# Three input projections as products of 512 columns, and two side jobs moved in the first experts of a mixture-of-experts layer

## The reference

```
h    = layer_norm(concat(meta, x))
proj = h @ w_in                          # q, k, v, og, a1, z, xbc, dt
gla  = rms_norm(gla_chunk_causal(q, k, v, log_a)) * silu(og)
ssd  = rms_norm((ssd_chunk_causal(...) + xs * d) * silu(z))
h    = layer_norm(alpha * h + concat(gla, ssd) @ w_out)
# top 4 of 32 experts per token; per expert e, for its tokens:
hid  = clamped_swiglu(x @ w_gate[e] + b_gate[e], x @ w_up[e] + b_up[e])
y   += gate * (hid @ w_down[e] + b_down[e])
out  = layer_norm(alpha * h + y)[:, 16:]
```

## Time and profile before

| | us |
|---|---|
| median of 3 runs | 1059.09 |
| the three runs | 1060.35, 1058.22, 1059.09 |
| the profiled execution | 1058.86 |
| its span in the profile | 1057.0 |
| TensorE busy | 1021.6 |
| VectorE busy | 228.6 |
| ScalarE busy | 143.9 |
| mean granted clock of TensorE | 0.991 |
| moved from HBM | 424.59 MB, 403 GB/s over the span |

### The profile page before, as it was taken

The page is one execution under the profiler, slowest core; times in us unless marked ns, Lnnn a source line. Parts: engine busy times, 40 slices in busy tenths (PEclk is TensorE's granted clock), DMA queues, the critical chain, the costliest instruction groups (busy, mean ns, idle before and its releaser), DMA issues.

```text
span 1057.0 us, 12137 instructions
## 1 busy us (share of the span) xinstructions
PE 1021.6 (97%) x5116; PEld 449.5 (43%) x5116; DVE 228.6 (22%) x495; ACT 143.9 (14%) x348; POOL 29.7 (3%) x50
## 2 busy tenths in 40 slices
PE   8999999999999999999999999999999999999997
PEld 7888764333333333333333333333333333333332
DVE  5453572111111111111111112211111111111112
ACT  3312331111111111011110111111111110011102
POOL 1230100000000000000000000000000000000000
PEclk9999999999999999999999999999999999999999
DMA  9894689999999999999999999999999999999995
GB/s 314 273 410 192 201 327 410 428 428 435 429 429 435 432 425 433 435 436 424 430 435 436 424 422 436 432 430 426 435 434 428 428 435 435 430 425 427 428 418 236
DMA packets 40011, 426.21 MB, mean 403 GB/s; under 512 B 6922, under 2 KB 19347, under 8 KB 23204
## 3 DMA queue, kind: packets, MB, share of 16 engines
q1 hardware_dynamic: 37940, 424.12, 95.6%
q10 hardware_dynamic: 2032, 1.53, 0.6%
HBM read 424.59 MB, written 1.05 MB: 403 GB/s over the span
## 4 chain that ended last, share of the span: by engine, by line
PE 72%; DMA 26%; ACT 1%; DVE 0%; issue 0%; SPq 0%; POOL 0%; DVEq 0%; POOLq 0%; ACTq 0%
PE bank L1200 30%; DMA ring<-in_moe_w_up 18%; PE bank L1251 15%; DMA ring<-in_moe_w_gate 8%; PE bank L1180 4%; PE bank L1172 4%; PE bank L856 3%; PE bank L871 2%; PE bank L1046 2%; PE bank L1034 1%; PE bank L988 1%; PE bank L1242 1%; PE bank L1120 1%; PE bank L949 1%; PE bank L1054 1%; PE bank L1220 1%
## 5 line engine op out<-in xcount | busy, mean ns | idle before, releaser
L1200 PE MATMUL bank<-ring,arena 128*64 128x512 f32 x1988 | 447.5, 603 | 23.8 <-DMA ring<-in_moe_w_up 20.3
L1200 PEld LDWEIGHTS bank<-ring,arena 128*64 128x64 f32 x1988 | 142.5, 139 | 298.7 <-issue 257.7
L1251 PE MATMUL bank<-ring,arena 128*64 128x512 f32 x1024 | 226.8, 595 | 1.5 <-issue 1.5
L1251 PEld LDWEIGHTS bank<-ring,arena 128*64 128x64 f32 x1024 | 71.5, 137 | 151.7 <-issue 150.2
L1641 DVE COPY arena<-bank 128x512 f32<-128x512 f32 x32 | 22.1, 692 | 326.0 <-PE bank L1251 326.0
L741 ACT ACTIVATE arena<-arena 128x512 f32<-128x512 f32 x32 | 20.1, 629 | 451.1 <-DVE arena L1628 451.1
L1180 PE MATMUL bank<-arena 64*128 64x512 f32 x256 | 72.0, 640 | 0.9 <-DVE arena L1641 0.9
L1172 PEld LDWEIGHTS bank<-arena 128*128 128x128 f32 x480 | 58.8, 196 | 22.8 <-issue 22.8
L1635 DVE TENSOR_SCALAR arena<-bank 128x512 f32<-128x512 f32 x32 | 22.1, 692 | 210.3 <-PE bank L1200 210.3
L752 ACT ACTIVATE arena<-bank 128x512 f32<-128x512 f32 x32 | 19.1, 597 | 337.4 <-PE bank L1242 337.4
L1172 PE MATMUL bank<-arena 128*128 128x128 f32 x480 | 64.5, 288 | 0.0
(11 more groups left out here) (281 smaller groups left out, 511.6 us busy)
## 6 DMA issues: line engine op xcount, KB each, us to landing
ring<-in_moe_w_down SPq DMA_DIRECT2D x25, 4096.0 KB, 29.6
ring<-in_moe_w_gate SPq DMA_DIRECT2D x24, 4096.0 KB, 25.4
ring<-in_moe_w_up SPq DMA_DIRECT2D x24, 4096.0 KB, 28.2
ring<-in_moe_w_gate SPq DMA_DIRECT2D x10, 2048.0 KB, 22.6
ring<-in_moe_w_up SPq DMA_DIRECT2D x10, 2048.0 KB, 15.2
ring<-in_moe_w_down SPq DMA_DIRECT2D x10, 2048.0 KB, 17.4
ring<-in_w_in SPq DMA_DIRECT2D x12, 1024.0 KB, 11.8
ring<-in_moe_w_gate SPq DMA_DIRECT2D x8, 1024.0 KB, 17.2
```

The lines of the kernel that those rows point to most:

```text
L1200: ins = mm(b[h * SL:(h + 1) * SL, :], (xA[pp], xB)[q][:, k, par * SL:(par + 1) * SL], columns(unit_at(m, kt), h), start=False, stop=kt == ...
L1251: ins = mm(bank[6][h * SL:(h + 1) * SL, :], hidT[:, kt % 4, (kt // 4) * SL:(kt // 4 + 1) * SL], unit_at(2, kt)[:, h * 512:(h + 1) * 512], ...
```

## The change

Seven edits in one. (1) `v`, `z` and `og` are loaded as 512 columns: the first transfer of a pair brings row groups 0 to 3 of all 512 columns, the second row groups 4 to 7 (`w_wide`); sizes, count and semaphores stay. (2) Their products are made 512 columns wide, 8 per token tile instead of 16 of 256 (`token_wide`); token tile 0 is now complete before tile 1 begins. (3) `meta_rows` reads the wide unit. (4) `counts()` writes bank 7 instead of bank 5. (5) `hidden_bias(0)` of expert 0 stands behind the first gathers instead of ahead of them. (6) `gate_transposes()`, its copy on ScalarE and the wait for it move from expert 0 to expert 3 (`BIASED`). (7) VectorE makes the list behind expert 0's first activation step, and TensorE waits for it behind `hidden(1)`.

```diff
+BIASED = UNROLL - 1
+WIDE = (U_V, U_Z, U_OG)
+        def w_wide(n):
+            return ring[:, n // 4, (n % 4) * HW:(n % 4 + 2) * HW].rearrange("p (k n) -> p k n", k=KT)
...
             for n, c0 in enumerate(W_ORDER):
-                sp.dma_start(w_unit(n), w_in[0, :, c0:c0 + 256].rearrange("(k p) n -> p k n", p=P)).then_inc(w_landed[n], 16)
+                if n in WIDE or n - 1 in WIDE:
+                    u = n if n in WIDE else n - 1
+                    c0, rows = W_ORDER[u], HALVES[n - u]
+                    sp.dma_start(w_wide(u)[:, rows, :], w_in[0, :, c0:c0 + 512].rearrange("(k p) n -> p k n", p=P)[:, rows, :]).then_inc(
+                        w_landed[n], 16)
+                else:
+                    sp.dma_start(w_unit(n), w_in[0, :, c0:c0 + 256].rearrange("(k p) n -> p k n", p=P)).then_inc(w_landed[n], 16)
...
-                if first:
+                if isinstance(n, int) and n == BIASED:
                     act.wait_ge(GT_ps, 1)
                     nc.scalar.activation(GT, bank[7][96:96 + NE, 0:SEQ], ACT.Copy).then_inc(GT_ok, 1)
...
+            def token_wide(out, n, t, kts):
+
+                for kt in kts:
+                    if kt % 4 == 0:
+                        pe.wait_ge(w_landed[n + kt // 4], 16)
+                    ins = mm(out, hT[:, kt, META + t * P:META + (t + 1) * P], w_wide(n)[:, kt, :], start=kt == 0, stop=kt == KT - 1)
+                return ins
...
-            token_major(bank[5][:, 0:256], U_V, 0)
+            token_wide(bank[5][:, :], U_V, 0, first_half)
...
-            token_major(bank[7][:, 0:256], U_V, 1)
+            token_wide(bank[5][:, :], U_V, 0, second_half).then_inc(v_ps, 1)
...
-            pe.wait_ge(w_landed[U_V + 1], 16)
-            for t, b in enumerate((bank[5], bank[7])):
-                token_major(b[:, 256:512], U_V + 1, t).then_inc(v_ps, 1)
-            meta_rows(bank[3][:, 0:HV], HV, [(U_V + g // 2, (g % 2) * HV) for g in range(4)]).then_inc(v_ps, 1)
+            token_wide(bank[7][:, :], U_V, 1, range(KT)).then_inc(v_ps, 1)
+            meta_rows(bank[3][:, 0:HV], HV, w_wide(U_V)).then_inc(v_ps, 1)
...
-            for hf in range(2):
-                n = U_Z + hf
-                pe.wait_ge(w_landed[n], 16)
-                for t in range(NT):
-                    for kt in range(KT):
-                        ins = mm(bank[(0, 5)[t]][:, hf * 256:(hf + 1) * 256], hT[:, kt, META + t * P:META + (t + 1) * P], wslot(n, kt),
-                                 start=kt == 0, stop=kt == KT - 1)
-                    if hf:
-                        ins.then_inc(z_ps, 1)
+            for t in range(NT):
+                token_wide(bank[(0, 5)[t]][:, :], U_Z, t, range(KT)).then_inc(z_ps, 1)
...
+            token_wide(bank[6][:, :], U_OG, 0, range(KT)).then_inc(og_ps, 1)
+            token_wide(bank[7][:, :], U_OG, 1, first_half)
+            pe.wait_ge(mix_y, 2)
+            mix_transposes(bank[0], z_t, (4, 5))
+            mix_transposes(bank[5], z_t, (6, 7))
+            token_wide(bank[7][:, :], U_OG, 1, second_half).then_inc(og_ps, 1)
...
-            hidden_bias(0, bank[4], 0, True)
...
+            hidden_bias(0, bank[4], 0, True)
...
-                    ins = mm(bank[5][0:1, 0:NE], ones_b[:, 0:1], maskb[:, t, :], start=t == 0, stop=t == 1)
+                    ins = mm(bank[7][0:1, SEQ:SEQ + NE], ones_b[:, 0:1], maskb[:, t, :], start=t == 0, stop=t == 1)
...
                 if first:
                     counts()
+                listing = isinstance(n, int) and n == BIASED
+                if listing:
                     gate_transposes()
-                else:
+                if not first:
                     pe.wait_ge(yd_ok, n)
...
-                if first:
-                    pe.wait_ge(list_ok, 1)
...
                 if first:
+                    pe.wait_ge(list_ok, 1)
+                if listing:
                     pe.wait_ge(GT_ok, 1)
...
                 ts(shuffled(a_c, 2), natural(bank[4][:, :], 2), LIMIT, None, ALU.min).then_inc(a_ok, 1)
+                if first:
+                    list_overflow()
```

More of the change, by code:

```diff
@@ L872, in token_major, with meta_rows @@
                 return ins
[L874 removed]
+            def token_wide(out, n, t, kts):
[4 more added lines that the diff above has]
+                return ins
+            def meta_rows(dst, cols, unit):
                 for kt in range(KT):
[L877 to L878 removed]
+                    for g, m in enumerate(MH):
+                        ins = mm(dst[m, :], hT[:, kt, 0:META], unit[:, kt, g * cols:(g + 1) * cols], start=kt == 0, stop=kt == KT - 1)
                 return ins
+            first_half, second_half = range(KT // 2), range(KT // 2, KT)
             pe.wait_ge(w_landed[U_K], 16)
@@ L884, in _ @@
             token_major(bank[4][:, 0:256], U_K, 0)
-            meta_rows(bank[1][:, 64:64 + HK], HK, [(U_K, g * HK) for g in range(4)])
+            meta_rows(bank[1][:, 64:64 + HK], HK, w_unit(U_K))
             pe.wait_ge(sT_ok, 1)
@@ L1612, in _, with list_overflow @@
             weigh(None, 0, 0)
-            dve.wait_ge(count_ps, 1)
-            for j in range(1, NJ):
-                ins = ts(flag[:, j - 1, :], bank[5][0:1, 0:NE], float(SL * j), None, ALU.is_gt)
-            link(ins)
-            flagf = flag[:, :, :].rearrange("p j e -> p (j e)")
-            link(nc.vector.tensor_tensor_scan(rank, flagf, ones[0:1, 0:3 * NE], 0.0, ALU.add, ALU.mult))
-            copy(xcount, rank[:, 3 * NE - 1:3 * NE]).then_inc(list_ok, 1)
+            def list_overflow():
+                dve.wait_ge(count_ps, 1)
+                for j in range(1, NJ):
+                    ins = ts(flag[:, j - 1, :], bank[7][0:1, SEQ:SEQ + NE], float(SL * j), None, ALU.is_gt)
+                link(ins)
+                flagf = flag[:, :, :].rearrange("p j e -> p (j e)")
+                link(nc.vector.tensor_tensor_scan(rank, flagf, ones[0:1, 0:3 * NE], 0.0, ALU.add, ALU.mult))
+                copy(xcount, rank[:, 3 * NE - 1:3 * NE]).then_inc(list_ok, 1)
             def tile(n, par, first, after, pair):
```

17 lines of the change are left out of this document (removed).

## The result

The changed kernel takes 1062.53 us in the median of 6 runs (1061.81 to 1064.37), the kernel before 1058.72 beside it (6 runs, 1058.22 to 1060.35). The ratio is 1.0035, 95% interval 1.0025 to 1.0046: 3.8 us slower. Forecast were 1057.7 us and a range from 1056.0 to 1059.6. The profiled execution took 1061.91 us, span 1060.2, clock 0.989.

What follows compares the result with a forecast made beforehand. The stream of expert weights was taken as the limit, continuous from about 149 us. Wide products 1.10 us plus expert 0's 0.3 gave 1.4 us off the median of 1059.09: 1057.7 us, range 1056.0 to 1059.6.

Steps and rivals of the forecast that it cites:

- the sum: Whole kernel: 1.10 us from the wide products plus 0.3 from expert 0, 1.4 us faster; chance 0.60.
- the signs that I listed as ways of being wrong: z or og records above 0.437 us, TensorE waiting for normed half, w_in or list, or last down product at half clock.
- the normed half: SSD half transposed three quarters into og: its input would stay ready with 1.1 us of cover left; nothing taken.
- The wide products: Projections v, z and og ahead of the stream: 512-column products save 0.47, 0.28 and 0.35 us, together 1.10, all on the chain.
- width buys nothing: Rival: the projections keep their time per column, only expert 0's 0.3 us is left, 1058.8 us; chance 0.14.
- Expert 0: From the counts to the up product TensorE saves 0.81 us, of which 0.3 reaches the end.
- Expert 3: The gates' transposes come back there, about 0.55 us, hidden by the continuous stream; nothing taken.
- the cascade paid in full: Rival: all 0.81 us of expert 0 reaches the stream, projections save 1.41; 2.2 us in all, 1056.9 us; chance 0.17.
- The principle that time ahead of the stream's release moves the end: What TensorE saves ahead of 146 us, where the half gate matrix is issued, moves stream and end by as much.
- the clock falls: Rival: half clock under the last down product at 1037.82 loses 1.75 us, 1059.4 us; chance 0.09.

Runs made afterwards that it cites:

- experiment 1: Changed kernel with eight dead fp32 products in the body of the branch not taken, moving its target by 32 instructions: 1064.27 us, ratio 1.0048.
- experiment 2: Kernel before with sixteen dead fp32 products in the body of the branch not taken, moving its target by 64 instructions: 1062.85 us, ratio 1.0042.
- experiment 9: Changed kernel with the 18 clock-keeping products at the start replaced by 8 wider ones, 40 instructions fewer: 1058.57 us, ratio 0.9997.
- experiment 8: Changed kernel repeated without further edits, beside three other kernels on one chip: 1064.28 us, ratio 1.0043.
- experiment 4: Kernel before with only the edits to experts 0 and 3, the projections left narrow: 1058.87 us, ratio 1.0000.
- experiment 11: Kernel before with the 18 clock-keeping products at the start replaced by 8 wider ones, 40 instructions fewer: 1059.05 us, ratio 1.0001.
- experiment 15: Changed kernel with 8 wide starting products and 44 tiny ones behind them, 136 instructions more ahead of the branch: 1060.23 us, ratio 1.0014.
- experiment 12: Kernel before with 14 dead fp32 products in the body of the branch not taken, moving its target by 56 instructions: 1060.48 us, ratio 1.0014.

## Why the prediction was wrong, step by step

**The step that failed** is the sum, which has no term for TensorE's own program. I read the diff for what is executed and took the place of the code for nothing; 191 instructions fewer ahead of a branch whose body is 320 long cost 4.38 us of tail, 2.75 us of stall and 1.63 of half clock behind it (experiments 1, 2 and 9). Of the signs that I listed as ways of being wrong none gave this away: z took 0.435 us a record, og's first group 0.4375, a hair over my 0.437 (10.50/24), and there was no wait for the normed half, none for the list, and the last down product ran at full clock, 7.09 us from 1036.58, as in the earlier trace rows.

**The wide products, 1.10 us forecast, 0.23 to 0.25 measured.** From the first convolution product to the half gate matrix it is 146.33 - 12.19 = 134.14 us before and 146.10 - 12.21 = 133.89 after. The same stretch is 134.13 or 134.14 us in each of the six profiles with narrow products and 133.89 or 133.90 in each of the eleven with wide ones, so this small gain is no chance. The error was in the reading: I divided the length of a group by its records. From start to start in the middle of a group it is 216 ns at 256 columns and 429 at 512, in v, z, og and the output projection alike; what a group takes beyond that are single steps about 0.1 us longer (320 ns among narrow records, 533 among wide ones), which the width doesn't remove. And I took the cheapest group of another projection for the target. The Trainium skill's 2.5 ns per matmul ("TensorE: Matmul & The Clock Gate", "Back-to-back issue gap", where it stands for an isolated matmul) gave 0.24, the rival "width buys nothing" 0; the page was right and my preference for the rows wrong.

**Expert 0: 0.81 us forecast on TensorE, 0.72 measured; 0.3 forecast at the end, nothing clear of noise. Expert 3: 0.55 forecast as hidden, 0.56 measured.** TensorE's down products (start, us) of experts 0, 3, 7 and 8, before, changed, and of experiment 2, which has no edits:

```profile
175.11 7.09 PE L1251 MATMUL bank<-ring,arena 128*64 128x512 f32 x32 [0.73 <-issue]
...
254.22 7.09 PE L1251 MATMUL bank<-ring,arena 128*64 128x512 f32 x32
...
363.44 7.09 PE L1251 MATMUL bank<-ring,arena 128*64 128x512 f32 x32
390.48 7.09 PE L1251 MATMUL bank<-ring,arena 128*64 128x512 f32 x32
```

```profile
174.16 7.09 PE L1257 MATMUL bank<-ring,arena 128*64 128x512 f32 x32 [0.73 <-issue]
...
253.83 7.09 PE L1257 MATMUL bank<-ring,arena 128*64 128x512 f32 x32
...
363.05 7.09 PE L1257 MATMUL bank<-ring,arena 128*64 128x512 f32 x32
389.52 7.09 PE L1257 MATMUL bank<-ring,arena 128*64 128x512 f32 x32
```

```profile
175.04 7.09 PE L1251 MATMUL bank<-ring,arena 128*64 128x512 f32 x32 [0.73 <-issue]
...
363.37 7.09 PE L1251 MATMUL bank<-ring,arena 128*64 128x512 f32 x32
389.74 7.09 PE L1251 MATMUL bank<-ring,arena 128*64 128x512 f32 x32
```

The changed kernel leads by 0.95 us, by 0.39 once expert 3 has taken its transposes back, and at expert 8, where the up products begin to wait for the stream, by 0.96. But there the kernel without edits, which was level until then (0.07), leads by 0.74. From that point on the spread of a microsecond between profiles hides the edits. The 1.25 us by which the changed profile's last scatter was early was therefore mostly chance: repeated (experiment 8) it came at 1045.87, 0.08 us later than in the profile of the kernel before. That is why I read "the cascade paid in full" out of the first pair of traces, and why it fell with the medians of experiments 4 and 9.

**The sum of 1.4 us** is, without the stall, 1058.57 against 1058.73 us: 0.2, with an interval from 1.3 us faster to 0.6 slower. Against experiment 11, with the same start, it is 0.48 us, and by the spread of the 11 runs of each, my estimate, anything from 1.5 us faster to 0.4 slower. The forecast gain lies at the edge of both; half a microsecond, what 0.25 and 0.3 make, fits either. The principle that time ahead of the stream's release moves the end is borne out, as far as the noise of about a microsecond allows (1.74 us lost there cost 1.66, experiment 15 against 9); there was only a quarter of a microsecond to move.

**The rival "the clock falls"** had nearly the right price in the wrong place: 1.63 us of half clock in the tail (1.75 forecast), behind a 2.75 us gap, where I looked for it under the last down product. That the prices are alike is luck: the products are others, and in another profile of the same kernel the clock cost 4.5 us (experiment 8).

What stays open: why a fetch takes 2.2 us in one profile and 3.0 in another; why the clock falls under the last products in some executions without a stall; and how much under a microsecond the edits are worth.

## What to carry to other kernels

Where an engine's program runs over several blocks, look at every branch that is taken over a long body near the end or on the critical path: its target and what follows should lie in the block behind the branch's own, and the branch's own block should have been entered well ahead (22 instructions were too few here, 70 were enough). A change that only removes instructions elsewhere can break this, and "issue" as the releaser of a gap that begins in the middle of a product is the sign. Before crediting or blaming an edit for a per cent, shift the code by dead instructions and measure again; and compare two traces only up to the point from which a saturated stream sets the time.

## What the runs showed of the hardware

- TensorE behind a taken branch to a block not yet there: 1.9 to 2.9 us of standing still, then a fallen clock, which cost another 1.6 to 4.7 us (tails of 10.8 to 14.4 against 6.92, less the stall).
- Block edges were 256 instructions of the count apart, and a stall's place followed the count to the instruction.
- From the start of the 16 KB packet to the first instruction behind the stall it was 2.2 to 3.0 us (eleven kernels), and a packet of that queue starts near the jump without a stall too.
- A fulfilled semaphore wait took TensorE 0.11 us per instruction (70 of them from 1.53 to 9.09 us); a tiny fp32 product of four instructions took 67 to 69 ns (88 records in 2.95 us, 56 in 1.94).
- Products of 512 columns in place of pairs of 256 saved 0.24 to 0.25 us over 96 records fewer, 2.5 to 2.6 ns each.
- Profiles of the kernel before with and without dead code in the branch's body (experiments 2 and 12) had their last scatter start between 1045.25 and 1045.79 us, those of the changed kernel (experiments 1 and 8 included) between 1044.54 and 1045.87, and the experts' edits alone at 1046.44, the latest of those with the old start: a difference of a microsecond between two profiles is no result here.
